# Token forms made in the tail before, output tiles finished in pairs, down chunks shifted by one pair, norm inside the third unit

## The chip, the cores and the metric

One core of a Trainium2 chip runs the whole program in one launch. TensorE (PE) multiplies, VectorE (DVE), ScalarE (ACT) and GpSimd (POOL) prepare operands and empty the accumulation banks, and SyncE (SP) issues every transfer. The metric is the device time of one execution in microseconds, the median of several; lower is better.

## The reference

The model is a decoder trunk of two layers over 512 tokens with 1024 features, in float32. Each layer is a token mixer between two half-step SwiGLU feed-forward networks (FFNs):

```python
def rms_norm(x, gain):
    y = x * lax.rsqrt(jnp.mean(x * x, axis=-1, keepdims=True) + RMS_EPS)
    return y * gain
def swiglu(x, w_gate, w_up, w_down):          # 1024 -> 2816 -> 1024
    return (jax.nn.silu(x @ w_gate) * (x @ w_up)) @ w_down
# x = x + 0.5 * swiglu(rms_norm(x))  before and after every mixer
```

Layer 0 mixes by dilated attention and causal pooling (one input and one output projection), layer 1 by an mLSTM with an input projection of 32 tiles and an output projection. So there are four FFNs, f = 0 to 3, in the order FFN 0, even mixer, FFN 1, FFN 2, odd mixer, FFN 3.

## The kernel before

**Layout and precision.** Activations stand with features on the partitions: `X` is 8 tiles of 128 features by 512 tokens. Every float32 operand is split into a high part (made by ACT) and a low part (made by DVE or POOL), and a product is three matmuls: high by high, high by low, low by high. A *unit* is one weight tile of 1024 by 128, loaded by SP into one of four ring slots (`RAW`), split into `HI` and `LO`, and multiplied with the 8 k-tiles of `XH` and `XL`: 24 matmuls of 512 columns into one bank (`products`, L504 to L506). A slot is loaded again when its unit is done.

**The FFN in blocks.** FFNs 1, 2 and 3 run in `block_ffn`. Of their 22 gate and up pairs the first 3 (`PLAIN`) are two plain units each, the other 19 are blocks: `block(p)` forms both outputs with seven half-size products in place of eight (L583 to L585: 84 matmuls of 256 columns). For it the kernel makes *token forms* `BF` and `BFL` once per FFN (`form_inputs` and `form_split` on ACT, `form` and `form_split` on DVE, a = 0 to 3, where form a needs the tiles a and 4 + a of X), and for each block sums of the weights (`ASR`, split to `ASH` and `ASL`). DVE puts the products together (`MID`), then `gate`, `up`. The sixteen blocks p = 4 to 19 are each followed by an *early* down product (`early`, L634 to L636: 24 matmuls of 512 columns, weights `DRAW` split to `DHI` and `DLO`), which adds 4 of the 22 hidden tiles to 2 of the 8 output tiles.

**The tail.** The last 6 hidden tiles go through the *tail*: 8 units of 6 k-tiles, one per output tile. After each, in this order on DVE: `residual_tile` (X, L1413), `new_x_tile` (XL, L1394, which waits for XH from ACT), then the split of the next weight tile (LO, L1448). ACT makes XH, the square and HI for each; POOL adds the squares.

**The start of a stage.** `two_units` runs the first two units side by side for 7 of the 8 k-tiles, so that the last tile of X may come late, and then their eighth; `norm(r)` adds up the squares with two matmuls (L533, L534), which wait for `SQL` (DVE L1399). ACT takes the root, DVE the reciprocal (`RSTD`), and only then can the banks of the first units be emptied. The order on DVE in `block_ffn` is written out by hand: form 0, SQL, form 1, split 0, form 2, split 1, norm, then splits, gates, ups, form 3 and the sums of block 3.

Each engine runs its list in order, so an instruction that waits holds up everything behind it on its engine.

Of the kernel before, what the change touches and what calls it, by code (L numbers as in the profile page):

```python
# [25 lines left out]
F32 = mybir.dt.float32  # L26
# [38 lines left out]
PLAIN = 3  # L65
BLOCKS = FT - PLAIN
EARLY = 16
TH_ = T // 2
# [73 lines left out]
def trunk(nc, xT, par_d, cst_d, hot_d, relb_d, w3_d, wgr_d, poolw_d, pick_d, gu_d, down_d, down2_d, ein_d, eout_d,  # L142
          oin_d, oout_d, skew_d, out_d):
    ctx = ExitStack()
    with ctx:
# [93 lines left out]
        BFR = at("BFR", [P, 4, 4, TH_], e0, 8 * TB)  # L239
        BFL = at("BFL", [P, 4, 4, TH_], e0, 8 * TB, F32R)  # L240
        ASR = at("ASR", [P, 2, 4, T], e0, 16 * TB)
        ASL = at("ASL", [P, 2, 4, T], e0, 16 * TB, F32R)
# [65 lines left out]
        sum_made, sum_hi, sum_lo = sem("sum_made"), sem("sum_hi"), sem("sum_lo")  # L308
        early_in, early_hi, early_lo, early_done, early_half, early_free = (
# [47 lines left out]
        def block_count(f, p):  # L357
            return BLOCKS * (f - 1) + p - PLAIN

        def early_count(f, p):  # L360
            return EARLY * (f - 1) + p - 4

        def has_early(p):
            return 4 <= p < 4 + EARLY

# [9 lines left out]
        def _(sp):  # L375
# [34 lines left out]
            def block_ffn(f, q0, after):  # L410
                base = 4 * q0

                def load_early(p):
                    e = early_count(f, p)
                    if p == 4:
                        sp.wait_ge(unit_done, base + 4)
                    if e:
                        sp.wait_ge(early_done, e)
                    m, c = 2 * ((p - 4) % 4), (p - 4) // 4
                    first = c % 2 * 4 * P  # L420
                    sp.dma_start(DRAW[:].rearrange("p (m c) -> p m c", m=2),
                                 down_d[f, 8 * (c // 2) + m:8 * (c // 2) + m + 2, :, first:first + 4 * P]
                                 .rearrange("m p c -> p m c")).then_inc(early_in, 16)

                for n in range(SLOTS, NU):
                    u = n if n < 2 * PLAIN else n ^ 1
                    load(q0 + n // 4, n % 4, gu_d[f, u])
                    p = n // 2 - 1
                    if n % 2 and has_early(p):
                        load_early(p)  # L430
                for m in range(KX):
                    load(q0 + (NU + m) // 4, m % 4, down2_d[f, m])
# [45 lines left out]
            projection(Q_OIN, 8, oin_d, oout_d)  # L478
            projection(Q_OOUT, 4, oout_d, gu_d[3])
            block_ffn(3, Q_FFN[3], None)  # L480
            for m in range(KX):

                sp.wait_ge(bank_free, 4 * Q_END - 8 + m + 5)
                sp.dma_start(out_d[:, m, :], X[:, m, :]).then_inc(out_done, 16)
# [4 lines left out]
        def _(pe):  # L489
# [26 lines left out]
            def x_tile_ready(r):  # L516
                return lambda k: pe.wait_ge(xl_ready, 8 * r + k + 1)

            def two_units(q, ready):

                for n0, n1 in ((0, KX - 1), (KX - 1, KX)):
                    for j in range(2):
                        pe.wait_ge(lo_ready, 4 * q + j + 1)
                        pe.wait_ge(bank_free, 4 * q + j + 1)
                        products(j, j, list(range(KX)), n0, n1, xh, xl, ready if j == 0 else None)
# [1591 lines left out]
```

## Time and profile before

| | |
|---|---|
| median of 3 runs | 2039.08 us (2036.6 to 2039.21) |
| profiled execution, own time | 2038.16 us |
| its span, first to last instruction | 2036.4 us |
| PE busy | 1988.9 us, 98% |
| DVE busy | 1372.5 us, 67% |
| ACT, POOL busy | 41%, 24% |
| mean granted TensorE clock | 0.995 |

Busy time of PE is not its peak, since matmuls overlap. In rows of a timeline the first number is the start in the span, the second the duration in microseconds, and a bracket at the end gives the idle time before the instruction and what ended it.

### The profile page before, as it was taken

The numbers are of one execution on the slowest core, as the hardware profiler recorded it, in microseconds if no ns is written. First come the engines' busy times: TensorE is split into PE (matmuls) and PEld (weight loads), VectorE is DVE, ScalarE is ACT, GpSimd is POOL, SyncE is SP. The second block draws the span as 40 slices with busy tenths as digits, with TensorE's granted clock in tenths as the row PEclk, the third lists the DMA queues.
The fourth block names the chain that finished last, engine by engine and source line by source line (L and its number), as shares of the span: only waits on it lengthen the run. The fifth ranks groups of instructions, "written<-read, shape, count | busy, mean of one in ns | idle before, by whom it ended". The sixth has DMA issues, their size and how long they took to land.

```text
span 2036.4 us, 27535 instructions
## 1 busy us (share of the span) xinstructions
PE 1988.9 (98%) x11150; PEld 1707.1 (84%) x11150; DVE 1372.5 (67%) x1752; ACT 838.3 (41%) x1200; POOL 492.1 (24%) x358
## 2 busy tenths in 40 slices
PE   7999999999999999999999999999998999999999
PEld 6888888876778999987899998877775788899998
DVE  6333333645498888868888886883468848888884
ACT  5323223524563343335334334554545335433342
POOL 1202112133231211222122122254025512211211
PEclk9999999999999999999999999999999999999999
DMA  5232223421123233322333333222200223223323
GB/s 177 93 102 95 93 93 131 149 83 52 53 85 111 97 101 104 104 83 83 105 103 104 96 112 99 94 86 83 79 1 1 73 93 104 94 95 113 95 93 104
DMA packets 61898, 189.25 MB, mean 93 GB/s; under 512 B 6096, under 2 KB 6352, under 8 KB 61776
## 3 DMA queue, kind: packets, MB, share of 16 engines
q1 hardware_dynamic: 61776, 187.52, 28.0%
q8 instruction: 89, 1.46, 0.3%
q14 instruction: 33, 0.27, 0.0%
HBM read 182.78 MB, written 4.72 MB: 92 GB/s over the span
## 4 chain that ended last, share of the span: by engine, by line
PE 82%; DVE 10%; ACT 3%; issue 2%; DMA 1%; POOL 1%; POOLq 0%; SPq 0%; DVEq 0%; ACTq 0%
PE BANKS L504 12%; PE BANKS L506 11%; PE BANKS L505 11%; PE BANKS L583 8%; PE BANKS L585 8%; PE BANKS L584 8%; PE BANKS L634 4%; PE BANKS L635 4%; PE BANKS L636 4%; DVE LO L1448 2%; PE BANKS L931 1%; ACT HI L1055 1%; DVE ASL L1493 1%; PE BANKS L757 1%; DVE SQ L1809 1%
## 5 line engine op out<-in xcount | busy, mean ns | idle before, releaser
L1386 DVE TENSOR_TENSOR LO<-RING,HI 128x1024 fp32r<-128x1024 f32 (+1 forms) x136 | 174.7, 1284 | 343.8 <-ACT HI L993 343.6
L504 PE MATMUL BANKS<-XH,HI 128*128 128x512 f32 x880 | 345.5, 393 | 11.5 <-DVE XL L1394 11.4
L505 PE MATMUL BANKS<-XL,HI 128*128 128x512 f32 x880 | 343.6, 391 | 0.0
L506 PE MATMUL BANKS<-XH,LO 128*128 128x512 f32 x880 | 343.5, 390 | 0.0
L1956 POOL TENSOR_TENSOR TMP<-TMP,RSTD 128x512 f32<-128x512 f32 x66 | 102.4, 1551 | 652.1 <-ACT TMP L1077 652.1
L993 ACT ACTIVATE HI<-RING 128x1024 fp32r<-128x1024 f32 (+1 forms) x144 | 150.2, 1044 | 228.7 <-DMA RING<-gu_dram 95.5
L504 PEld LDWEIGHTS BANKS<-XH,HI 128*128 128x128 f32 x880 | 165.9, 189 | 51.8 <-DVE LO L1386 11.0
L583 PE MATMUL BANKS<-BF,ASH 128*128 128x256 f32 x684 | 195.0, 285 | 4.6 <-DVE ASL L1493 4.4
L506 PEld LDWEIGHTS BANKS<-XH,LO 128*128 128x128 f32 x880 | 165.8, 188 | 34.9
L505 PEld LDWEIGHTS BANKS<-XL,HI 128*128 128x128 f32 x880 | 166.0, 189 | 34.0
L585 PE MATMUL BANKS<-BF,ASL 128*128 128x256 f32 x684 | 194.3, 284 | 0.0
L584 PE MATMUL BANKS<-BFL,ASH 128*128 128x256 f32 x684 | 194.3, 284 | 0.0
L1448 DVE TENSOR_TENSOR LO<-RING,HI 128x1024 fp32r<-128x1024 f32 (+2 forms) x152 | 158.8, 1045 | 31.3 <-ACT HI L1055 31.1
L1077 ACT ACTIVATE TMP<-TMP 128x512 f32<-128x512 f32 x66 | 41.7, 632 | 302.0 <-DVE TMP L1503 301.7
L634 PE MATMUL BANKS<-HH,DHI 128*128 128x512 f32 x384 | 152.3, 397 | 6.1 <-DVE DLO L1552 6.1
L635 PE MATMUL BANKS<-HL,DHI 128*128 128x512 f32 x384 | 151.9, 395 | 0.0
L636 PE MATMUL BANKS<-HH,DLO 128*128 128x512 f32 x384 | 151.3, 394 | 0.0
L1493 DVE TENSOR_TENSOR ASL<-ASR,ASH 128x1024 fp32r<-128x1024 f32 x114 | 141.5, 1243 | 0.0
L583 PEld LDWEIGHTS BANKS<-BF,ASH 128*128 128x128 f32 x684 | 132.2, 193 | 5.7 <-DVE ASL L1493 5.7
L583 PE MATMUL BANKS<-XH,HI 128*128 128x256 f32 x456 | 129.3, 284 | 4.1 <-DVE LO L1448 4.0
L584 PEld LDWEIGHTS BANKS<-BFL,ASH 128*128 128x128 f32 x684 | 132.2, 193 | 0.0
L585 PEld LDWEIGHTS BANKS<-BF,ASL 128*128 128x128 f32 x684 | 132.1, 193 | 0.0
(254 smaller groups left out, 4729.1 us busy)
## 6 DMA issues: line engine op xcount, KB each, us to landing
RING<-gu_dram SPq DMA_DIRECT2D x176, 512.0 KB, 3.4
DRAW<-down_dram SPq DMA_DIRECT2D x48, 512.0 KB, 3.8
RING<-oin_dram SPq DMA_DIRECT2D x32, 512.0 KB, 3.4
RING<-down_dram SPq DMA_DIRECT2D x32, 384.0 KB, 3.1
RING<-down_dram SPq DMA_DIRECT2D x16, 512.0 KB, 3.4
RING<-ein_dram SPq DMA_DIRECT2D x16, 512.0 KB, 3.4
RING<-oout_dram SPq DMA_DIRECT2D x16, 512.0 KB, 3.4
RING<-eout_dram SPq DMA_DIRECT2D x8, 512.0 KB, 3.8
```

The lines of the kernel that those rows point to most:

```text
L504: pe.matmul(PS[bank][:], HI[j][:, c], hi(k), start=(n == 0), stop=False)
L505: pe.matmul(PS[bank][:], HI[j][:, c], lo(k), start=False, stop=False)
L506: last = pe.matmul(PS[bank][:], LO[j][:, c], hi(k), start=False, stop=(n == len(order) - 1))
L583: pe.matmul(out, w_hi[:, c], x_hi(k), start=(k == 0), stop=False)
L584: pe.matmul(out, w_hi[:, c], x_lo(k), start=False, stop=False)
L585: last = pe.matmul(out, w_lo[:, c], x_hi(k), start=False, stop=(k == 3))
L634: pe.matmul(bank, DHI[:, col], HH[:, h, :], start=(k == 0), stop=False)
L635: pe.matmul(bank, DHI[:, col], HL[:, h, :], start=False, stop=False)
L636: last = pe.matmul(bank, DLO[:, col], HH[:, h, :], start=False, stop=(k == 3))
L1386: dve.tensor_tensor(LO[j][:, 0:kt * P], RAW[j][:, 0:kt * P], HI[j][:, 0:kt * P].bitcast(F32), ALU.subtract).then_inc(lo_ready, 1)
L1448: dve.tensor_tensor(LO[j][:, cols], RAW[j][:, cols], HI[j][:, cols].bitcast(F32), ALU.subtract).then_inc(lo_ready, 1)
L1493: dve.tensor_tensor(ASL[:, p % 2, 2 * i:2 * i + 2, :], ASR[:, p % 2, 2 * i:2 * i + 2, :], ASH[:, p % 2, 2 * i:2 * i + 2, :].bitcast(F32), ...
```

## The change

- `PLAIN` becomes `(None, 4, 3, 3)`: FFN 1 has four plain pairs and 18 blocks, FFNs 2 and 3 stay at three and 19.
- Early down products begin with the first block (`PLAIN[f]`) and still last sixteen blocks. `LATE = (None, 6, 7, 7)`: in FFNs 2 and 3 the tail takes 7 hidden tiles, and the first four early products take 3 instead of 4. Chunks that cross the border of two weight arrays are loaded in two transfers, and each late weight tile of FFNs 2 and 3 in two (64 KB and 384 KB, the first counted on `late_in`).
- From FFN 1's tail on, output tiles are finished in the order `PAIRED = (0, 4, 1, 5, 2, 6, 3, 7)`, also in both output projections' consumers, and PE takes the k-tiles in that order.
- Forms 0 to 2 and the splits 0 and 1 of FFN 2 are made in the tail of FFN 1, those of FFN 3 in the second half of the odd mixer's output projection (`forms_behind`). `BFR`/`BFL` and `ASR`/`ASL` exchange their places in memory.
- `start_of_stage` replaces `two_units` and `norm`: the norm's two matmuls stand behind the first 3 k-tiles of the third unit, in all six stages that have a norm.
- At the end of the even mixer two weight splits stand behind the last tile of XL instead of between the tiles.

```diff
-PLAIN = 3
-BLOCKS = FT - PLAIN
+PLAIN = (None, 4, 3, 3)
 EARLY = 16
+LATE = (None, 6, 7, 7)
+PAIRED = (0, 4, 1, 5, 2, 6, 3, 7)
...
+        def early_tiles(f, p):
+            c, first = (p - PLAIN[f]) // 4, FT - LATE[f] - 12
+            return range(first) if c == 0 else range(first + 4 * c - 4, first + 4 * c)
...
+            def start_of_stage(q, r):
                 for n0, n1 in ((0, KX - 1), (KX - 1, KX)):
                     for j in range(2):
...
+                        products(j, j, x_order(r), n0, n1, xh, xl, x_tile_ready(r) if j == 0 else None)
+                unit_with_norm(q, r)
+
+            def unit_with_norm(q, r):
+                pe.wait_ge(lo_ready, 4 * q + 3)
+                pe.wait_ge(bank_free, 4 * q + 3)
+                products(2, 2, list(range(KX)), 0, 3, xh, xl)
+                norm(r)
+                products(2, 2, list(range(KX)), 3, KX, xh, xl)
...
+            def forms_behind(f, m):          # ACT: form_inputs and form_split, DVE: form and form_split
+                if m in (2, 4, 6):
+                    form(f, m // 2 - 1)
+                if m in (3, 5):
+                    form_split(f, m // 2 - 1)
...
                 for m in range(KX):                       # the tail of block_ffn on DVE
                     residual_tile(q0 + (NU + m) // 4, m % 4, r, m, 0.5)
                     if m < 4:
-                        split(NU + 4 + m, slice(0, 6 * P))
+                        split(NU + 4 + m, late)
                     elif after:
                         split(NU + 4 + m, whole)
+                    if f == 1:
+                        forms_behind(2, m)
...
+                else:                                     # the start on DVE for f = 2 and 3
+                    squares_low(now)
+                    form_split(f, 2)
+                    form(f, 3)
+                    form_split(f, 3)
+                    norm(now)
+                    split(4, whole)
+                    gate(0)
+                    up(0)
+                    split(5, whole)
+                    gate(1)
+                    sums_first(first)
+                    up(1)
...
                     if m:                                 # the end of the even mixer on DVE
                         new_x_tile(2, m - 1)
-                        if m % 2 == 0:
-                            if m == 2:
-                                dve.wait_ge(lo_ready, N_ATTN + 4)
-                            split_unit(N_ATTN + m // 2 + 3)
+                        if m == 2:
+                            dve.wait_ge(lo_ready, N_ATTN + 4)
+                            split_unit(N_ATTN + 4)
+                        elif m == 4:
+                            split_unit(N_ATTN + 5)
+                split_unit(N_ATTN + 6)
+                split_unit(N_ATTN + 7)
```

## Rows read from the trace of the kernel before

**Rows 1.** The page's first part: busy time and share, PE.

```profile
PE 1988.9 (98%) x11150; PEld 1707.1 (84%) x11150; DVE 1372.5 (67%) x1752; ACT 838.3 (41%) x1200; POOL 492.1 (24%) x358
```

**Rows 2.** Waits of PE: total us, times, longest.

```profile
PE BANKS L504 <- DVE XL L1394: 11.4, 2, 10.2
...
PE BANKS L634 <- DVE DLO L1552: 6.1, 3, 2.0
PE BANKS L583 <- DVE ASL L1493: 4.4, 3, 1.7
PE BANKS L583 <- DVE LO L1448: 4.0, 2, 2.7
...
PE BANKS L533 <- DVE SQL L1399: 2.0, 3, 1.3
...
PE BANKS L504 <- POOL HL L1958: 1.0, 3, 0.3
```

**Rows 3.** Windows at FFN starts: length; PE, PEld, DVE, ACT, POOL; clock; DMA.

```profile
567.72:632.85 65.13, 58.11 (x322) 50.04 (x321) 58.61 (x71) 34.19 (x46) 18.77 (x12) 0.97 0.27 89
919.39:991.05 71.66, 64.42 (x339) 55.54 (x338) 61.24 (x74) 36.38 (x49) 19.09 (x13) 0.93 0.27 89
1680.26:1746.57 66.31, 61.60 (x339) 53.30 (x338) 57.65 (x71) 33.02 (x45) 17.50 (x11) 0.97 0.28 95
```

**Rows 4.** Timeline of PE at the start of FFN 2.

```profile
919.39 0.39 PE L504 MATMUL BANKS<-XH,HI 128*128 128x512 f32 x1
919.62 0.39 PE L505 MATMUL BANKS<-XL,HI 128*128 128x512 f32 x1
...
957.24 0.39 PE L583 MATMUL BANKS<-XH,HI 128*128 128x256 f32 x1 [2.72 <-DVE LO L1448]
...
960.59 0.58 PE L583 MATMUL BANKS<-BF,ASH 128*128 128x256 f32 x1 [1.02 <-DVE ASL L1493]
...
981.43 0.28 PE L584 MATMUL BANKS<-BFL,HI 128*128 128x256 f32 x1
981.55 0.28 PE L585 MATMUL BANKS<-BF,LO 128*128 128x256 f32 x1
983.87 0.50 PE L634 MATMUL BANKS<-HH,DHI 128*128 128x512 f32 x1 [2.04 <-DVE DLO L1552]
...
985.42 0.63 PE L634 MATMUL BANKS<-HH,DHI 128*128 128x512 f32 x1
985.85 0.63 PE L635 MATMUL BANKS<-HL,DHI 128*128 128x512 f32 x1
```

**Rows 5.** Timeline of DVE, tail of FFN 1 and start of FFN 2.

```profile
922.14 0.75 DVE L1394 SCALAR_TENSOR_TENSOR XL<-X,PAR,XH 128x512 fp32r<-128x512 f32 x1 [0.80 <-ACT XH L1000]
...
926.53 0.75 DVE L1394 SCALAR_TENSOR_TENSOR XL<-X,PAR,XH 128x512 fp32r<-128x512 f32 x1 [0.79 <-ACT XH L1000]
...
929.44 0.47 DVE L1454 SCALAR_TENSOR_TENSOR BFR<-X,PAR,MID 128x256 f32<-128x256 f32 x1
...
930.96 0.68 DVE L1399 TENSOR_TENSOR SQL<-SQ,SQH 128x512 fp32r<-128x512 f32 x1
...
933.77 1.22 DVE L1466 TENSOR_TENSOR BFL<-BFR,BF 128x1024 fp32r<-128x1024 f32 x1
...
957.10 3.43 DVE L1493 TENSOR_TENSOR ASL<-ASR,ASH 128x1024 fp32r<-128x1024 f32 x2
```

**Rows 6.** Timeline of POOL, start of FFN 2.

```profile
957.32 2.14 POOL L1956 TENSOR_TENSOR TMP<-TMP,RSTD 128x512 f32<-128x512 f32 x1 [1.22 <-ACT TMP L1077]
```

**Rows 7.** Timeline of DVE, end of the odd mixer's output projection.

```profile
1685.00 1.22 DVE L1386 TENSOR_TENSOR LO<-RING,HI 128x1024 fp32r<-128x1024 f32 x1 [2.10 <-ACT HI L993]
```

**Rows 8.** Timeline of DVE, blocks 20 and 21 of FFN 2.

```profile
1227.30 0.42 DVE L1518 TENSOR_TENSOR MID<-BANKS,MID 128x256 f32<-128x256 f32 x1 [2.11 <-PE BANKS L585]
...
1239.31 0.41 DVE L1518 TENSOR_TENSOR MID<-BANKS,MID 128x256 f32<-128x256 f32 x1
```

**Rows 9.** DMA issues: KB each, median us to landing.

```profile
DRAW<-down_dram SPq DMA_DIRECT2D x48, 512.0 KB, 3.8
```

More of the change, by code:

```diff
@@ L852, in odd_mixer @@
                 q0 = Q_OIN
-                two_units(q0, x_tile_ready(4))
-                norm(4)
-                for j in range(2, SLOTS):
-                    unit(q0, j, KX, xh, xl)
+                start_of_stage(q0, 4)
+                unit(q0, 3, KX, xh, xl)
                 def bank(item):
@@ L1115, in block_ffn @@
+                split(2 * first, whole)
+                sums_split(first, 0)
+                sums_split(first, 1)
+                split(2 * first + 1, right)
+                silu(first - 1, 1.0)
+                h_high(first - 1)
+                for p in range(first, FT):
                     nxt = p + 1 if p + 1 < FT else None
                     copy_one(p)
-                    if p > PLAIN and not has_early(p - 1):
+                    if p > first and not has_early(f, p - 1):
                         h_high(p - 1)
@@ L1576, in block_ffn @@
-                form_split(3)
-                sums_first(PLAIN)
-                up(1)
-                sums_second(PLAIN)
-                sums_third(PLAIN)
-                dve.wait_ge(sum_made, 3 * block_count(f, PLAIN) + 3)
-                gate(2)
-                split(6, whole)
-                sums_split(PLAIN, 0)
-                sums_split(PLAIN, 1)
-                split(7, right)
-                up(2)
-                for p in range(PLAIN, FT):
+                now, first, late = (2, 3, 5)[f - 1], PLAIN[f], slice(0, LATE[f] * P)
@@ new lines, in block_ffn @@
+                if f == 1:
+                    form(f, 0)
+                    squares_low(now)
+                    form(f, 1)
+                    form_split(f, 0)
+                    form(f, 2)
+                    form_split(f, 1)
+                    norm(now)
+                    split(4, whole)
+                    gate(0)
+                    form(f, 3)
+                    form_split(f, 2)
+                    up(0)
+                    split(5, whole)
+                    gate(1)
+                    form_split(f, 3)
+                    up(1)
+                    split(6, whole)
+                    split(7, whole)
+                    gate(2)
+                    up(2)
+                    sums_first(first)
+                else:
+                    squares_low(now)
+                    form_split(f, 2)
+                    form(f, 3)
+                    form_split(f, 3)
+                    norm(now)
+                    split(4, whole)
+                    gate(0)
+                    up(0)
+                    split(5, whole)
+                    gate(1)
+                    sums_first(first)
+                    up(1)
@@ L1589, in block_ffn @@
+                sums_second(first)
+                sums_third(first)
+                dve.wait_ge(sum_made, 3 * block_count(f, first) + 3)
+                gate(first - 1)
+                split(2 * first, whole)
+                sums_split(first, 0)
+                sums_split(first, 1)
+                split(2 * first + 1, right)
+                up(first - 1)
+                for p in range(first, FT):
                     nxt = p + 1 if p + 1 < FT else None
-                    if has_early(p):
+                    if has_early(f, p):
@@ L1633, in block_ffn @@
                         gate(p)
[L1634 removed]
+                        split(NU + 2, late)
                         up(p)
[L1636 removed]
+                split(NU + 3, late)
                 for m in range(KX):
```

304 lines of the change are left out of this document (165 added, 139 removed).

## The prediction

> **What bounds the kernel now.** I read the page first: PE is busy for 1988.9 us, 98% of the span [rows 1], so a gain can only come from the 47 us in which it is idle, from a lower clock, or from fewer matmuls. Next PE's waits [rows 2]: apart from the wait for the first data (10.2 of the 11.4 for XL) the larger ones name DVE, and the three for DLO, the three for ASL and the two for LO belong to `block_ffn`, which runs three times. The windows of the three starts [rows 3] show the same: DVE is busy 58.6 of 65.1, 61.2 of 71.7 and 57.7 of 66.3 us while PE goes without work, and the mean clock is 0.97, 0.93, 0.97. In steady blocks no such wait occurs. The bound is therefore DVE's list at three starts, PE everywhere else.
>
> **The rates.** From neighbouring starts [rows 4]: a 512-column matmul starts every 0.2275 us (919.39 to 919.62, rounded), a 256-column one every 0.12, and at half clock a 512-column one every 0.43. So a unit is 24 x 0.2275 = 5.46, a block 84 x 0.12 = 10.08, a plain pair 10.92. Reading the start-to-start times over each start, what exceeds those rates (idle time, restart of about 0.1, lower clock) is 10.2 us for FFN 1, 12.6 for FFN 2, 7.6 for FFN 3. About 1.6, 3.5 and 1.5 of it is clock; the windows' clocks times their lengths give 2, 5 and 2 [rows 3], coarser because rounded.
>
> **FFN 1.** The fourth plain pair gives DVE one more pair (10.9 us of PE work for about 3.5 us of its own: two splits, a gate, an up) before block sums are wanted, and it removes block 3 with its sums. The forms stay at this start. Going through DVE's list with the old durations, the split sums of block 4 are ready about 1 us before PE wants them; the early product's DLO comes about 0.5 us late, because the second weight tile of block 5 is loaded only after the last plain unit. The XL wait of 1.2 [rows 2] goes with the weight split (1.1 us on DVE) moved behind the XL tiles; 0.15 is left. Cost: 10.92 - 10.08 = 0.84 more matmul time. Gain 10.2 - 0.15 - 0.6 - 0.84 = 8.6; it would be 7.0 if one half-clock stretch came back, 9.2 with no wait left.
>
> **FFN 2, the doubtful part.** The forms go into FFN 1's tail, and there DVE is not idle in a useful sense: tile by tile it goes X, wait for XH, XL, wait for HI, LO, next X, a chain of 4.1 to 4.4 us per tile between DVE and ACT, while PE needs 18 x 0.2275 = 4.1. It ends late as it is: PE begins FFN 2 at 919.39 [rows 4], the seventh XL tile starts at 922.14, the eighth at 926.53 [rows 5]. A form is 929.44 to 930.96 = 1.52 us, a form split 1.22 less 0.09 of overlap = 1.13. They stand between LO and the next X, so they add to the chain: 2 forms and 2 splits = 5.3 before the seventh tile, a third form = 6.8 before the eighth. The seventh XL is then ready at 922.14 + 0.75 + 5.3 = 928.2; PE wants it after six k-tiles, at 919.39 + 18 x 0.2275 = 923.5. **PE waits 4.7 us at a place where it waits for nothing now**, then 0.4 for the eighth (928.2 + 0.7 + 4.8 = 933.7 against 934.1). A wait of 2.0 is followed by half clock here (983.87, then 0.43 from 985.42) [rows 4], so I add one such stretch, 1.6. Behind that, DVE's list from form 0 to the last split sum takes 929.44 to 960.53 [rows 5], and is 6.8 shorter by the same forms while it starts 6.8 later: the second product of block 3, now at 960.59, comes at about 961.4. So the waits up to there (norm, LO, ASL: 6.5 with restarts and 0.5 of clock) buy nothing. What is gained lies behind: the half clock from 960.6 on (1.7 with restart), 0.4 at MID, 2.3 for DLO, 1.4 of clock, since early products already follow block 3 and DVE keeps its lead; less 0.8 for the later product and about 0.3 for DLO in block 3. Gain 4.8. Bounds: 11.5 if the tail had room, 0 if the forms took longer and the clock stayed low longer (rivals).
>
> At the last step DVE and POOL matter together: two ASL splits of 1.22 each take 3.43 [rows 5] beside POOL's 2.14 us multiply [rows 6], so about 1.1 is lost to it. In the tail a form follows LO, after POOL's add has ended, and I charge nothing. The Trainium skill (SBUF — State Buffer, Who interferes with whom) says that a DVE instruction with two SBUF inputs and a GpSimd instruction that reads SBUF exclude each other for a whole instruction, whoever starts first. The trace agrees in the two rows named. By that rule alone each of the three forms could lose up to 1.1 in the tail and FFN 2's gain would be 1.5 instead of 4.8; the order in the list speaks against it.
>
> **FFN 3.** Here the forms go behind the output projection's units of 24 matmuls. DVE has 2.10 us of idle time before each LO [rows 7], more than a form (1.52), so the delay doesn't add up: only the last form moves the eighth XL by 1.5, and the two side-by-side units hide that. DVE's list at the start is 6.8 shorter, the norm comes 9 x 0.2275 = 2.05 later than now, and the sums must wait for the fourth unit's slot to be reloaded; split sums are ready about 0.7 before PE's second product. The waits for LO, ASL, MID and DLO with their clock go, about 0.6 at the first DLO stays. Gain 7.0; 5.4 with one half-clock stretch.
>
> **Norm in the third unit.** Where PE waits for SQL it now has 2.05 us of work. Start of the kernel and odd mixer: the SQL waits are 2.0 in all, 1.3 of them FFN 2's [rows 2], so 0.7, with restarts 1.2. The cover: the root comes up to 2 us later, but between norm and the fifth unit lie 39 matmuls = 8.9 us, against about 8 us for root, reciprocal, first scaling and split. Were the cover gone, each of six norms would cost at most 2.05.
>
> **Tail of FFNs 2 and 3.** With 7 k-tiles the two first units run 36 matmuls before they need the last hidden tile instead of 30: of three waits for HL two go, 0.7, with restarts 1.2. Matmuls are the same in number. But three blocks without early product now follow each other (19, 20, 21) in place of two. Such a block takes DVE 1227.30 to 1239.31 = 12.0 us [rows 8] against PE's 10.08, so DVE falls 1.9 behind once more; block 21's split sums are late by 0 to 1.9, I take 1.2: twice, minus 2.4.
>
> **Transfers.** Four early chunks in each of FFNs 2 and 3 come in two pieces. One piece lands in 3.8 us [rows 9]; the split of DRAW starts some 5 us after the buffer is free, so I charge nothing; two pieces strictly after each other would land at 7.6 and cost about 1 us each, 8 in all.
>
> **Sum.** 8.6 + 4.8 + 7.0 + 1.2 + 1.2 - 2.4 = 20.4 us. The profiled execution took 2038.16, its span 2036.4 with 1.8 around it: 2017.8. The median of the runs lies 0.9 above it: 2018.7, I say 2018.5.
>
> **Rivals.**
> - *The tail has room* (0.12): the chain with ACT absorbs the forms, no wait at the seventh XL. For it: DVE is idle 0.5 to 0.8 twice a tile. Against it: those gaps are waits within the chain, not at its end. FFN 2 gains 11.5: 2012.
> - *The tail costs more* (0.17): the wait for XL is 7 or more and the clock is low for twice as long, FFN 2 gains 0: 2023.5.
> - *Covers fail elsewhere* (0.08): transfers in two pieces late (8 us) or block 21 late by the full 1.9: 2027.
> - *No difference* (0.04): a moved wait simply turns up at the next early product in all three FFNs, since DVE is busy 90% of each start. Against it: block 3's sums and the forms do leave those windows. 2036.
> - *Slower* (0.04): the two-piece transfers. They decide from the point where the second piece lands more than 2.6 us later than DRAW's split can bear, 20.4 / 8; at one full extra latency each with PE's clock halved after each wait (2 + 1.6 + 1 per block) the loss is 37: 2055. No row shows two pieces on one counter.
>
> The forecast itself has 0.55, its own range 2013 to 2023. The range 2011 to 2027 takes in the first three rivals' times and leaves out no more than 0.2. A difference under 0.2% (4 us) can't be told from none: faster 0.91, same 0.05, slower 0.04.
>
> **What the profile after should show.** PE waits: a new one for XL of 4 to 5 us in FFN 2's first unit (right) or none (the tail has room); ASL, LO and DLO together under 4 us instead of 14.5; no SQL. PE clock 1.0 in FFN 1's and FFN 3's starts, below it in FFN 2's. An ASL wait near block 21 of FFNs 2 and 3. FFN 1's window from its first unit to the first full block after the first early product shorter by about 8.6. The prediction is wrong if early products wait for DHI (transfers), or if FFNs 1 and 3 still show half clock at their starts.

## The result and the profile after

The changed kernel takes **2022.93 us** (median of 4 runs, 2021.86 to 2023.61). The kernel before took 2038.8 beside it (4 runs, 2036.6 to 2039.21). The ratio is 0.9924, its 95% interval 0.9907 to 0.9941: 15.9 us faster where 20.4 was forecast. The profiled execution took 2022.40 us, 15.8 less than that of before, so its trace can stand for the difference.

The page's first part and PE's waits (total us, times, longest), to be laid beside [rows 1] and [rows 2]:

```profile
PE 1982.1 (98%) x11114; PEld 1701.4 (84%) x11114; DVE 1364.1 (68%) x1742; ACT 836.8 (41%) x1197; POOL 492.4 (24%) x358
```

```profile
PE BANKS L538 <- DVE XL L1466: 15.0, 3, 10.1
...
PE BANKS L626 <- DVE ASL L1573: 3.9, 4, 1.2
...
PE BANKS L676 <- DVE DLO L1633: 1.8, 3, 0.9
...
PE BANKS L626 <- DVE LO L1546: 0.5, 2, 0.3
PE BANKS L538 <- POOL HL L2065: 0.3, 1, 0.3
```

ASL, LO and DLO came to 14.5 us and now come to 6.2; SQL is gone, of three HL waits one is left. XL grew from 11.4 to 15.0: 10.1 is the first data as before, the new part is one wait of 4.35 us. Of the 3.9 for ASL, 2.4 stand at block 21 of FFNs 2 and 3, where nothing waited before. The windows of the three starts (length; PE, PEld, DVE, ACT, POOL; clock; DMA), against [rows 3]:

```profile
566.98:625.26 58.28, 56.53 (x286) 47.84 (x285) 52.15 (x61) 31.74 (x43) 16.11 (x11) 1.00 0.29 100
911.77:982.28 70.51, 64.55 (x352) 55.31 (x350) 57.97 (x71) 35.48 (x47) 19.23 (x12) 0.98 0.29 94
1669.42:1732.33 62.91, 62.00 (x352) 54.42 (x350) 51.36 (x62) 29.16 (x40) 16.88 (x11) 1.00 0.32 105
```

FFN 1's window is 65.13 - 58.28 = 6.85 us shorter. The two others hold 12 matmuls more of 512 columns than before (two early products of 18 in place of one of 24), 2.7 us, so their lengths can't be compared directly. FFN 2's wait and its clock, in PE's timeline (start, duration, bracket: idle time before and what ended it):

```profile
915.62 0.39 PE L540 MATMUL BANKS<-XH,LO 128*128 128x512 f32 x1
920.36 0.80 PE L538 MATMUL BANKS<-XH,HI 128*128 128x512 f32 x1 [4.35 <-DVE XL L1466]
...
922.66 0.63 PE L540 MATMUL BANKS<-XH,LO 128*128 128x512 f32 x1
923.09 0.60 PE L538 MATMUL BANKS<-XH,HI 128*128 128x512 f32 x1
923.51 0.40 PE L539 MATMUL BANKS<-XL,HI 128*128 128x512 f32 x1
```

922.66 to 923.09 is the 0.43 of half clock, from 923.51 on the full one is back.

As in the prediction, I read the starts of all matmuls of one profiled execution and summed what exceeds the three rates of the prediction. This sum is called *excess* below: it holds idle time, the restart after it and lower clock. In these terms the gain is made up so:

| term | before | after | gain | forecast |
|---|---|---|---|---|
| FFN 1's start, less 0.84 for the longer pair | 9.99 | 2.29 | 6.9 | 8.6 |
| FFN 2's start | 12.62 | 8.77 | 3.85 | 4.8 |
| FFN 3's start | 7.45 | 1.32 | 6.1 | 7.0 |
| norm, start of the kernel and odd mixer | | | 1.4 | 1.2 |
| HL waits in two tails | | | 1.15 | 1.2 |
| block 21, FFNs 2 and 3 | 0 | 3.6 | -3.6 | -2.4 |
| sum | | | 15.8 | 20.4 |

### The profile page after: what moved, and what is told of

Read it like the earlier page. It is cut to its first block, busy times and chain, and to the rows that moved or that the text cites. A ratio compares the mean times of both kernels' runs of the same rounds, so it can differ in the third digit from the quotient of the medians.

```text
span 2020.7 us, 27444 instructions
## 1 busy us (share of the span) xinstructions
PE 1982.1 (98%) x11114; PEld 1701.4 (84%) x11114; DVE 1364.1 (68%) x1742; ACT 836.8 (41%) x1197; POOL 492.4 (24%) x358
## 4 chain that ended last, share of the span: by engine, by line
PE 85%; DVE 9%; ACT 2%; issue 2%; POOL 1%; DMA 1%; SPq 0%; DVEq 0%; POOLq 0%; ACTq 0%
PE BANKS L538 13%; PE BANKS L539 13%; PE BANKS L540 13%; PE BANKS L626 9%; PE BANKS L628 9%; PE BANKS L627 9%; PE BANKS L676 4%; PE BANKS L677 4%; PE BANKS L678 4%; PE BANKS L970 1%; DVE LO L1546 1%; DVE LO L1457 1%; DVE XC L1858 1%; PE BANKS L798 1%; DVE SQ L1914 1%
## 5 line engine op out<-in xcount | busy, mean ns | idle before, releaser
L538 PE MATMUL BANKS<-XH,HI 128*128 128x512 f32 x896 | 352.4, 393 | 15.1 <-DVE XL L1466 15.0
L539 PE MATMUL BANKS<-XL,HI 128*128 128x512 f32 x896 | 350.3, 391 | 0.0
L540 PE MATMUL BANKS<-XH,LO 128*128 128x512 f32 x896 | 350.2, 391 | 0.0
L1546 DVE TENSOR_TENSOR LO<-RING,HI 128x1024 fp32r<-128x1024 f32 (+3 forms) x152 | 163.0, 1072 | 34.6 <-ACT HI L1116 34.5
L676 PE MATMUL BANKS<-HH,DHI 128*128 128x512 f32 x368 | 144.1, 392 | 1.8 <-DVE DLO L1633 1.8
L677 PE MATMUL BANKS<-HL,DHI 128*128 128x512 f32 x368 | 143.7, 391 | 0.0
L678 PE MATMUL BANKS<-HH,DLO 128*128 128x512 f32 x368 | 143.2, 389 | 0.0
L1116 ACT ACTIVATE HI<-RING 128x1024 fp32r<-128x1024 f32 (+3 forms) x152 | 126.3, 868 | 16.6 <-DMA RING<-down_dram 16.6
L538 PE MATMUL BANKS<-HH,HI 128*128 128x512 f32 x336 | 130.8, 389 | 0.3 <-POOL HL L2065 0.3
L539 PE MATMUL BANKS<-HL,HI 128*128 128x512 f32 x336 | 130.7, 389 | 0.0
```

Of the source, the lines that this page charges most:

```text
L538: pe.matmul(PS[bank][:], HI[j][:, c], hi(k), start=(n == 0), stop=False)
L539: pe.matmul(PS[bank][:], HI[j][:, c], lo(k), start=False, stop=False)
L540: last = pe.matmul(PS[bank][:], LO[j][:, c], hi(k), start=False, stop=(n == len(order) - 1))
L676: pe.matmul(bank, DHI[:, col], HH[:, h % 8, :], start=(k == 0), stop=False)
L677: pe.matmul(bank, DHI[:, col], HL[:, h % 8, :], start=False, stop=False)
L678: last = pe.matmul(bank, DLO[:, col], HH[:, h % 8, :], start=False, stop=(h == tiles[-1]))
```

## The experiments

Twelve kernels ran. The e's below are edits of the changed kernel, but for e9, which is an edit of e7, and e12, one of e9. Times of one kernel spread over 1.8 to 5.5 us (up to 6.6 for the kernel before), and much of that is not at the places studied. Between 1290 and 1600 us PE works on the mLSTM of the odd mixer, which no edit touches, and the excess there was 49.2 to 54.2 us by profiled execution. These are windows of that stretch with seven late tiles in FFN 1 (first row) and with four plain pairs and the gate moved (second):

```profile
1290.00:1600.00 310.00, 298.23 (x1363) 229.19 (x1362) 208.93 (x226) 157.02 (x239) 111.42 (x88) 0.98 0.16 51
```

```profile
1290.00:1600.00 310.00, 297.07 (x1382) 228.75 (x1381) 211.47 (x227) 156.91 (x240) 120.14 (x92) 1.00 0.16 53
```

The clock is 0.98 against 1.00 of 310 us; from 1500 to 1600 us alone it is 0.93 and 1.00, so some 14 us at half clock against none. The other executions lie between, and their excess in the mLSTM follows the clock. The runs of one kernel show the same: those of e2 took 2023.01 us at a mean clock of 0.997 and 2017.67 at 1.0. So a kernel's place is read from its excess at the starts, and its time says whether that holds. The excess is that of one execution each. Where two kernels have the same instructions at a start it agrees within 0.3 us, even at FFN 2's start (8.77 to 8.96 in the changed kernel, e4, e5 and e11), although half clock behind the XL wait lasts twice as long in e4. The kernels ran in five groups on several chips, the changed one, e1 to e4, e5 to e8, e9 to e11 and e12, each group beside the kernel before: across groups the ratios compare better than the medians. All in us; ratios are to the kernel before, each beside its own runs of it; "block 21" is the excess at that block of FFN 2 (FFN 3 has as much again).

| kernel | median | ratio, 95% | FFN 1 | FFN 2 | block 21 | mLSTM | FFN 3 |
|---|---|---|---|---|---|---|---|
| before | 2038.8 | 1 | 9.99 | 12.62 | 0 | 50.2 | 7.45 |
| changed | 2022.93 | 0.9924 (0.9907 to 0.9941) | 2.29 | 8.77 | 1.8 | 50.3 | 1.32 |
| e1 | 2021.44 | 0.9916 (0.9902 to 0.9929) | 2.11 | 7.04 | 1.8 | 53.2 | 1.41 |
| e2 | 2020.75 | 0.9909 (0.9895 to 0.9922) | 2.02 | 6.01 | 1.8 | 54.2 | 1.34 |
| e3 | 2028.97 | 0.9954 (0.9940 to 0.9967) | 2.19 | 12.50 | 0 | 50.5 | 3.93 |
| e4 | 2032.34 | 0.9970 (0.9957 to 0.9982) | 8.71 | 8.96 | 1.8 | 49.2 | 1.43 |
| e5 | 2024.72 | 0.9932 (0.9915 to 0.9948) | 2.14 | 8.89 | 1.8 | 51.4 | 1.48 |
| e6 | 2017.99 | 0.9897 (0.9880 to 0.9913) | 1.89 | 3.60 | 1.8 | 51.7 | 1.41 |
| e7 | 2012.39 | 0.9868 (0.9852 to 0.9885) | 2.02 | 1.11 | 0 | 51.8 | 0.97 |
| e8 | 2017.95 | 0.9891 (0.9875 to 0.9908) | 1.87 | 4.73 | 0 | 54.2 | 1.05 |
| e9 | 2014.41 | 0.9888 (0.9872 to 0.9903) | 2.38 | 1.17 | 0 | 49.9 | 1.34 |
| e10 | 2025.65 | 0.9941 (0.9927 to 0.9954) | 2.59 | 9.65 | 1.8 | 51.8 | 2.02 |
| e11 | 2023.98 | 0.9931 (0.9917 to 0.9944) | 2.13 | 8.79 | 1.8 | 50.6 | 2.57 |
| e12 | 2011.11 | 0.9863 (0.9846 to 0.9880) | 1.66 | 0.63 | 0 | 50.3 | 0.11 |

(Four plain pairs cost 0.84 of matmul time per FFN: in FFN 1 in all kernels but before and e4, in FFNs 2 and 3 in e7, e8, e9 and e12.)

**e1: FFN 2's forms back at its own start.**

```diff
-                    if f == 1:
-                        forms_behind(2, m)
...
+                elif f == 2:
+                    form(f, 0)
+                    squares_low(now)
+                    form(f, 1)
+                    form_split(f, 0)
+                    form(f, 2)
+                    form_split(f, 1)
+                    norm(now)
+                    split(4, whole)
+                    gate(0)
+                    form(f, 3)
+                    form_split(f, 2)
...
```

The first two lines are in the tail, on ACT and DVE; the others are DVE's list at the start, and ACT's changes likewise.

> The changed kernel, but all four token forms of FFN 2 are made at the start of FFN 2 again (none in FFN 1's tail); everything else stays, the order of tiles and the shifted down chunks included. In the changed kernel FFN 2's start costs 8.9 us over the rates, 4.9 of it the wait for the seventh XL tile and about 1.3 the half clock behind it. Theory (the forms in this tail nearly pay for themselves and no more): the XL wait and its clock go, but DVE's list at the start is 6.8 us longer, so LO, ASL and DLO are late by 2 to 3 us each again; excess of 11 to 12 us, 2 to 3.5 us slower than the changed kernel, 2025 to 2026.5. Rival 1 (the forms in the tail are a net loss, the other parts gain): excess 7 or less, 2021 or less. Rival 2 (they are the whole gain of FFN 2 and more): 4 us or more slower, above 2027.

My theory fell. The first rival came nearest and missed both its bounds by a hair (7.04 for 7, 2021.44 for 2021): the excess is 1.7 less than in the changed kernel. The XL wait is gone. In its place stand one of 1.29 for the bank of the third pair's first unit (DVE's gate 0) and one for LO with half clock behind it. In FFN 2 neither ASL nor DLO is late:

```profile
948.88 0.58 PE L626 MATMUL BANKS<-XH,HI 128*128 128x256 f32 x1 [2.73 <-DVE LO L1561]
```

The times alone (ratios 0.9916 and 0.9924) can't tell the two kernels apart. By the excess the forms in FFN 1's tail save nothing.

The XL rows show why. With forms in the tail (changed kernel), then without (e1):

```profile
902.84 0.75 DVE L1466 SCALAR_TENSOR_TENSOR XL<-X,PAR,XH 128x512 fp32r<-128x512 f32 x1 [0.79 <-ACT XH L1039]
908.10 0.75 DVE L1466 SCALAR_TENSOR_TENSOR XL<-X,PAR,XH 128x512 fp32r<-128x512 f32 x1 [0.79 <-ACT XH L1039]
914.03 0.75 DVE L1466 SCALAR_TENSOR_TENSOR XL<-X,PAR,XH 128x512 fp32r<-128x512 f32 x1 [0.79 <-ACT XH L1039]
919.55 0.75 DVE L1466 SCALAR_TENSOR_TENSOR XL<-X,PAR,XH 128x512 fp32r<-128x512 f32 x1 [0.79 <-ACT XH L1039]
925.47 0.75 DVE L1466 SCALAR_TENSOR_TENSOR XL<-X,PAR,XH 128x512 fp32r<-128x512 f32 x1 [0.80 <-ACT XH L1039]
```

```profile
905.01 0.75 DVE L1481 SCALAR_TENSOR_TENSOR XL<-X,PAR,XH 128x512 fp32r<-128x512 f32 x1 [0.79 <-ACT XH L1039]
909.40 0.75 DVE L1481 SCALAR_TENSOR_TENSOR XL<-X,PAR,XH 128x512 fp32r<-128x512 f32 x1 [0.79 <-ACT XH L1039]
913.78 0.75 DVE L1481 SCALAR_TENSOR_TENSOR XL<-X,PAR,XH 128x512 fp32r<-128x512 f32 x1 [0.79 <-ACT XH L1039]
918.17 0.75 DVE L1481 SCALAR_TENSOR_TENSOR XL<-X,PAR,XH 128x512 fp32r<-128x512 f32 x1 [0.79 <-ACT XH L1039]
```

Without forms a tile takes 4.39 us where PE takes 4.10: DVE falls behind by 0.29 per tile anyway. With forms the steps are 5.26, 5.93, 5.52 and 5.92: the two splits add 0.87 and 1.13, the two forms 1.54 and 1.53, so nearly all of their own length (1.13 and 1.52). None of them lost a further 1.1, as a DVE split does beside POOL's multiply in [rows 5] and [rows 6]. The last XL stands 13.7 us behind PE's first matmul of FFN 2 (911.77) with forms, 6.9 without (911.29): 6.8 later, as the prediction had it.

**e2: seven late tiles in FFN 1 too.** `EFIRST` says where early products begin; the high part of hidden tiles 11, 15 and 19 is made one block later.

```diff
-LATE = (None, 6, 7, 7)
+LATE = (None, 7, 7, 7)
+EFIRST = (None, 4, 3, 3)
...
-                    if has_early(f, p):
+                    if not high_later(f, p):
                         h_high(p)
```

> The changed kernel with 7 late hidden tiles in FFN 1 too, so that PE needs 21 matmuls = 4.78 us for each tile of the tail in place of 4.10 (as many matmuls in all; its early products still begin with block 4, and three high parts of hidden tiles are made one block later so that their slots are free). Theory (the XL wait of 4.5 us is the excess of DVE's chain of 4.1 to 4.4 us per tile plus forms over PE's time per tile): each of four or more tiles gives DVE 0.68 us more, the wait for the seventh tile falls by about 2.7 to 1.8, the HL wait in FFN 1's tail (0.5, with restart 0.6) goes, the half clock goes or halves: 3.7 to 5 us faster than the changed kernel, 2018 to 2019.5. Rival 1 (the chain hangs on PE's own time through the banks, so it stretches along): wait stays above 4, only the HL wait goes, 2022.3. Rival 2 (twelve more two-piece transfers or the late high parts cost): waits for DHI or HL in FFN 1's blocks, above 2023.

```profile
917.11 0.50 PE L543 MATMUL BANKS<-XH,HI 128*128 128x512 f32 x1 [1.58 <-DVE XL L1471]
```

The wait fell from 4.35 to 1.58 (1.8 expected), there is no half clock behind it, the HL wait is gone, nothing waits for DHI: 3.4 us less excess from 700 us on. The wait is thus DVE's chain against PE's time per tile: it fell by 2.77 where four tiles of 0.68 more make 2.7. The median fell by 2.2 only, where 3.7 to 5 were expected, and the intervals overlap; 3.9 of the profiled execution went to the mLSTM.

**e3: no shift of the down chunks.**

```diff
-LATE = (None, 6, 7, 7)
+LATE = (None, 6, 6, 6)
+EFIRST = (None, 4, 4, 4)
```

> The changed kernel without the shift of the down chunks: early products begin with block 4 in all three FFNs, four hidden tiles each, 6 late tiles, one transfer per chunk. Theory (three blocks in a row without early product cost DVE its lead, wherever they lie; DVE takes 12.0 us for such a block, PE 10.08): the waits at block 21 (1.85 and 1.84 with restarts) go and the first DLO waits (0.9 and 1.2) move, two HL waits come back (1.2), but block 3 now puts DVE 1.9 us further behind at block 4, twice: about the same as the changed kernel, 2022 to 2024. Rival 1 (the shift is only a cost): 4 us faster, 2018.5. Rival 2 (the shift is what gains behind block 3): waits of over 2 us each for DLO at block 4 with half clock behind them, 4 us or more slower, above 2027.

```profile
973.49 0.39 PE L627 MATMUL BANKS<-BF,HI 128*128 128x256 f32 x1 [0.75 <-DVE MID L1605]
...
977.22 0.50 PE L677 MATMUL BANKS<-HH,DHI 128*128 128x512 f32 x1 [2.04 <-DVE DLO L1634]
...
1728.89 0.50 PE L677 MATMUL BANKS<-HH,DHI 128*128 128x512 f32 x1 [2.04 <-DVE DLO L1634]
```

```profile
973.02 0.41 DVE L1605 TENSOR_TENSOR MID<-BANKS,MID 128x256 f32<-128x256 f32 x1
973.36 1.21 DVE L1547 TENSOR_TENSOR LO<-RING,HI 128x1024 fp32r<-128x1024 f32 x1
974.49 0.41 DVE L1611 TENSOR_TENSOR MID<-BANKS,MID 128x256 f32<-128x256 f32 x1
974.82 1.21 DVE L1574 TENSOR_TENSOR ASL<-ASR,ASH 128x1024 fp32r<-128x1024 f32 x1
975.96 1.21 DVE L1634 TENSOR_TENSOR DLO<-DRAW,DHI 128x1024 fp32r<-128x1024 f32 x1
```

The second rival stood, but for the half clock that it saw behind the waits: there is none. The waits at block 21 went, which shows that three blocks in a row make them and two don't; but 2.04 us for DLO came back, the same figure as in [rows 2] (three waits, longest 2.0) and [rows 4]. It is the same whatever went before, because PE and DVE meet late in the block: PE waits for DVE's MID (973.49), has 1.41 us of work left from there (to its last start at 974.90), and DVE's list from that MID to the end of DLO takes 4.15 (973.02 to 977.17). In FFN 1 of the kernel before the same stretches are 621.91 to 623.32 for PE and 621.44 to 625.59 for DVE. The shift is worth 6 us by the times and 3.9 by the excess. Up to 1.3 of the 3.9 may be chance: half clock lasts twice as long behind the XL wait here. It does so in e4 too, which has the shift, and there the FFN costs 0.2 more in the end.

**e4: three plain pairs in FFN 1.**

```diff
-PLAIN = (None, 4, 3, 3)
+PLAIN = (None, 3, 3, 3)
+EFIRST = (None, 4, 3, 3)
...
```

The lists of ACT and DVE at this start lose the fourth pair with it.

> The changed kernel with three plain pairs in FFN 1 as before (forms at its start, early products from block 4). The changed kernel's FFN 1 start costs 2.6 us over the rates and 0.84 for the longer pair. Theory (the fourth pair is what gains there, by 10.9 us of PE work against 3.5 of DVE's own): of the 10.2 us before, only the XL wait (0.7) and the gap at norm are gone, waits for LO, ASL and DLO are back; 5 to 6.5 us slower than the changed kernel, 2028 to 2029.5. Rival (norm inside the third unit and the moved weight splits make up most of it): 1 to 2 us slower, 2024 to 2025.

By the excess the theory stood: 8.71 against 2.29 + 0.84, 5.6 us for the fourth pair; LO, ASL and DLO (2.04 again) are late as before. The profiled execution took 2027.79, 5.4 more than the changed kernel's. The five others took 2031 to 2033, so the median is 9.4 us slower, more than the 5 to 6.5 expected. Their mean clock was 0.994 to 0.996, that of the profiled one 0.997, which can make 2 to 6 us; where it was lower the one trace doesn't show.

**e5: norm before the third unit.**

```diff
-                products(2, 2, list(range(KX)), 0, 3, xh, xl)
                 norm(r)
-                products(2, 2, list(range(KX)), 3, KX, xh, xl)
+                unit(q, 2, KX, xh, xl)
```

> The changed kernel with the norm's two matmuls before the third unit again, in all six stages. Theory (SQL comes up to 2 us after the first two units and three k-tiles of work cover it): waits for SQL return, 0.7 us in all at the start of the kernel and the odd mixer and about 1.3 in FFN 2, with restarts 2 to 2.5; no wait is less than in the changed kernel, since the root's chain had room. 1 to 2.5 us slower, 2024 to 2025.5. Rival (the root and what hangs on it was late by those 2 us, the block sums above all): the waits at the starts, 1.3 us at block 4 of FFN 1 and 2.7 behind the norm in FFN 2, shrink by more than SQL costs: same or faster, 2020 to 2022.9.

```profile
24.29 0.47 PE L573 MATMUL BANKS<-SQH,SELR 128*128 128x512 f32 x1 [1.15 <-DVE SQL L1468]
```

1.8 us slower by the medians, with overlapping intervals. The trace has 1.4 at norm in the kernel's start, but only 0.4 to 1.0 over the first 40 us (3.3 in e5 and in the kernel before, 2.3 to 2.9 in the others); 0.3 in the even mixer and 0.1 in FFN 2. None of the starts got better, so norm inside the third unit is covered, as the theory had it. The rest of the theory failed: it had waits for SQL in FFN 2 (1.3) and in the odd mixer too, and there is only the one above. In FFN 2 PE is itself late by the XL wait. In e1, where it isn't, DVE ends SQL at 923.29, 1.1 us after PE begins the third unit, and there the new place covers a wait.

**e6: both, seven late tiles and forms at the start.** Edits of e1 and e2 together.

> Seven late tiles in FFN 1 and the forms of FFN 2 at its start, three plain pairs there. FFN 2's start cost 8.8 us over the rates in the changed kernel, 7.0 with its forms at the start, 6.0 with seven late tiles and the forms in the tail. Theory (with 4.78 us per tile DVE leaves the tail earlier against PE, and a list without forms in the tail ends it without any XL wait): excess 4 to 5.5, 2018.5 to 2020. Rival (DVE's list from the start of FFN 2 on sets the sums whatever the tail): excess 7 as with six late tiles, 2021.

FFN 2's start costs 3.60, less than the theory's 4 to 5.5. The XL and bank waits are gone, LO keeps 1.46. What FFN 2 lacked was time to leave FFN 1's tail, not room in its own list: against e1 the slower tail saves 3.4 us, and against e2 (6.01) the forms back in the list save 2.4.

**e7 and e8: four plain pairs everywhere, FFN 2's forms at the start or in the tail.**

```diff
-PLAIN = (None, 4, 3, 3)
+PLAIN = (None, 4, 4, 4)
...
-LATE = (None, 6, 7, 7)
+LATE = (None, 7, 7, 7)
+EFIRST = (None, 4, 4, 4)
...
-                if f == 1:
+                if f < 3:
                     form(f, 0)
...
```

The last lines are in e7 only: there FFNs 1 and 2 share one list.

> Four plain pairs, early products from block 4 and seven late tiles in all three FFNs; FFN 1's and FFN 2's forms at their own start, FFN 3's in the output projection. Theory (10.9 us of PE work against 3.5 of DVE's is what a start wants; two blocks without early product in a row cost no wait, three do): FFN 2's start costs 2.4 us as FFN 1's, no wait at block 21, FFN 3's start under 0.8; plus 0.84 of matmuls twice: 9 to 10 us faster than the changed kernel, 2013 to 2014. Rival (the fourth pair only moves the wait to the first early product): waits for DLO of 1 us or more in FFNs 2 and 3, 2017 or more.

> The same with FFN 2's forms in the tail of FFN 1, as in the changed kernel. Theory (with four plain pairs the list at the start has room, so a form in the tail only costs): an XL wait of 1.8 us and 0.5 and 1.0 behind it stay, all that the forms' removal from the list gives is under 2.3; same as the kernel with forms at the start or up to 2.5 us slower, 2014 to 2016. Rival (the list at the start is still what is late): faster than that kernel, 2012 or less.

PE's waits in e7, XL with only the first data of the kernel (10.1) and 0.5 in FFN 1:

```profile
PE BANKS L543 <- DVE XL L1473: 10.6, 2, 10.1
...
PE BANKS L631 <- DVE ASL L1580: 1.6, 2, 1.0
...
PE BANKS L681 <- DVE DLO L1640: 1.1, 2, 0.8
```

2012.39, 10.5 faster than the changed kernel where 9 to 10 were expected. e8 has 3.6 us more excess in FFN 2, with the XL wait of 1.54; more than the 2.5 expected at most, the same sign. Its median is 5.6 above e7's, and the profiled executions differ by 6.5, 2.4 of it in the mLSTM. The forms in this tail are a loss in all three pairs of kernels, of 1.7 (e1), 2.4 (e6 against e2) and 3.6 us (e7 against e8): the more room the start has, the greater.

**e9 and e10: the gate behind the split sums**, on e7 and on the changed kernel.

```diff
-                gate(first - 1)
                 split(2 * first, whole)
                 sums_split(first, 0)
                 sums_split(first, 1)
+                gate(first - 1)
```

> The kernel with four plain pairs, seven late tiles and FFN 2's forms at its start, and in addition DVE's gate of the last plain pair placed behind the two splits of the first block's sums in all three FFNs (it stood ahead of the weight split before them). In that kernel PE still waits 1.18 and 0.74 for the second ASL split, which takes 2.32 us beside POOL's multiply of 1.94 where it takes 1.22 alone, and POOL's multiply follows from this gate. Theory (DVE and POOL hold each other up there, and the gate stands ahead of what PE wants first): both ASL waits go, 2.0 with restarts, and DLO is up to 0.7 earlier: 2 to 3.5 us faster, 2009 to 2010.5. Rival (the multiply meets another DVE instruction later and the first early product waits by as much more): DLO waits grow by 1 each, no gain, 2012 to 2013.

> The same single edit on the changed kernel (four, three, three plain pairs). There PE waits 1.17 for ASL in FFN 1, 0.74 in FFN 2, 0.15 to 0.26 at the fourth product of block 3 in FFNs 2 and 3, and 0.4, 0.8 and 1.1 for DLO. Theory as above: the ASL waits go in FFNs 1 and 2 (2.1 with restarts) and DLO gains up to 0.5 each: 2 to 3.5 us faster than the changed kernel, 2019.5 to 2021. That would say that 1.8 of the gain missing in FFN 1 was lost to POOL. Rival: no gain, DLO waits grow, 2022.9.

DVE and POOL in the changed kernel, FFN 1 (the first row is both splits together, the second the later of them):

```profile
607.05 3.46 DVE L1573 TENSOR_TENSOR ASL<-ASR,ASH 128x1024 fp32r<-128x1024 f32 x2
608.18 2.32 DVE L1573 TENSOR_TENSOR ASL<-ASR,ASH 128x1024 fp32r<-128x1024 f32 x1
```

```profile
607.49 1.94 POOL L2063 TENSOR_TENSOR TMP<-TMP,RSTD 128x512 f32<-128x512 f32 x1 [3.50 <-ACT TMP L1126]
```

And in e10, DVE (the first row is both splits together), POOL and PE:

```profile
606.18 2.35 DVE L1573 TENSOR_TENSOR ASL<-ASR,ASH 128x1024 fp32r<-128x1024 f32 x2
...
611.21 0.69 DVE L1592 TENSOR_TENSOR TMP<-BANKS,TMP 128x512 f32<-128x512 f32 x1 [1.48 <-POOL TMP L2063]
```

```profile
609.88 1.30 POOL L2063 TENSOR_TENSOR TMP<-TMP,RSTD 128x512 f32<-128x512 f32 x1 [6.16 <-ACT TMP L1126]
```

```profile
612.89 0.39 PE L626 MATMUL BANKS<-BF,ASH 128*128 128x256 f32 x1 [0.75 <-ACT MID L1137]
```

The mechanism was right: apart from each other the split takes 1.2 us and the multiply 1.30, together 2.32 and 1.94, and the ASL wait in FFN 1 is gone (in e10 that of 0.6 in FFN 2 stays, against the forecast). The gain was not there. DVE now stands idle for 1.48 before `up`, until POOL is done, and ACT copies product one to MID only behind the high part that waits for this `up`. The wait moved from the second product to the fourth and to DLO. The excess at the three starts is 1.9 us more in e10 than in the changed kernel and 0.8 more in e9 than in e7. The medians are 2.7 and 2.0 above theirs, with overlapping intervals, where 2 to 3.5 less were expected. The rival stood in both (no gain), with ACT's queue as a part that I had not seen.

**e11: FFN 3's forms at its own start.** The edit of e1 for f == 3; `forms_behind(3, ...)` leaves the output projection.

> The changed kernel with all forms of FFN 3 at FFN 3's own start (none behind the output projection). FFN 3's start costs 1.4 us over the rates in the changed kernel; FFN 2's costs 7.0 with its forms at the start and the same lists. Theory (behind units of 24 matmuls DVE has 2.1 us of idle time per tile, so the forms cost nothing there and their whole relief of the start is kept): excess 6 to 7.5, 4.5 to 6 us slower than the changed kernel, 2027.5 to 2029. Rival (as in FFN 2 the relief is given back, here by later XL and norm): within 1.5 us, 2021.5 to 2024.5.

Excess 2.57 against 1.32, 1.3 us and the rival's range; the theory had 6 to 7.5. That is the second surprise: three forms and two splits, 6.8 us of DVE's list, are hidden almost whole in the list at this start. DVE's rows show where. First the changed kernel, then e11:

```profile
1683.73 3.35 DVE L1475 RECIPROCAL RSTD<-RSTD 128x512 f32<-128x512 f32 x1 [0.89 <-ACT RSTD L1053]
...
1696.06 1.23 DVE L1555 TENSOR_TENSOR ASR<-RING 128x1024 f32<-128x1024 f32 x1 [2.61 <-DMA RING<-gu_dram]
```

```profile
1683.66 3.35 DVE L1490 RECIPROCAL RSTD<-RSTD 128x512 f32<-128x512 f32 x1
```

The reciprocal begins at the same time with the forms in the list and without. Without them DVE waits before it for ACT, and 2.61 us more for the transfer of the weight tile that the sums need.

**e12: the first early split ahead**, on e9.

```diff
                 split(2 * first + 1, right)
+                early_high(first)
                 silu(first - 1, 1.0)
+                copy_one(first)
                 h_high(first - 1)
...
                 split(2 * first + 1, right)
+                early_split(first)
                 up(first - 1)
```

The first part is ACT's list, the second DVE's. For this block the three calls fall away at their later places.

> The kernel with four plain pairs and the gate behind the split sums, and in addition: ACT copies the first block's product one (MID) before it makes the last plain pair's high part instead of behind it, and the first early product's DHI and DLO are made by ACT and DVE before the last plain pair's silu and up, in the 1.5 us in which DVE waits for POOL there. Without these two PE waited 0.9 and 0.4 for MID and 0.8, 0.8 and 1.2 for DLO, and the ASL waits had gone. Theory (what bounds a start now is DVE's list up to the first DLO, in which POOL costs either 1.1 of longer splits or 1.5 of idle time; an edit that only moves the wait gains nothing, one that fills the idle time does): MID and DLO waits of the first early products go, PE's excess behind 560 us falls from 5.5 (4.7 with the gate ahead) to about 1.5; 3 to 4 us faster than the kernel with the gate ahead, if the projections' own spread of 2 us allows to see it: 2008.5 to 2011. Rival (the split ahead delays the up and with it the sums of the second block, whose split sums are then late): an ASL or LO wait of 1 us at the second block in each FFN, 2011 to 2013.

```profile
PE BANKS L543 <- DVE XL L1479: 10.9, 2, 10.5
...
PE BANKS L681 <- DVE DLO L1646: 1.1, 2, 0.6
```

DVE's rows in FFN 1:

```profile
610.29 0.95 DVE L1646 TENSOR_TENSOR DLO<-DRAW,DHI 128x768 fp32r<-128x768 f32 x1
612.43 0.69 DVE L1605 TENSOR_TENSOR TMP<-BANKS,TMP 128x512 f32<-128x512 f32 x1 [1.19 <-POOL TMP L2080]
```

DLO now comes before `up`, in place of 619.15 in e9. The idle time before `up` is not gone: POOL's multiply lies beside this split, `up` comes 0.6 later than in e9 (612.43 for 611.83), and 1.19 of the 1.48 is left. No wait for ASL or MID over 0.3 is left, and the first early product waits no more in any FFN; FFNs 1 and 2 wait 0.57 for DLO at the second one, a mild form of the rival. Excess at the three starts is 2.40 against 4.10 in e7. The median 2011.11 is the lowest of all, 1.3 below e7 where 3 to 4 were expected, and the intervals don't separate them; against the changed kernel it is 11.8 us.

## Why the prediction was right, and where it was off

The time (2022.93) lies in the range and is nearer to 2018.5 than to the kernel before; every term came with its sign. The mechanism came too: a wait for the seventh XL tile of 4.35 us (4 to 5 forecast), clock 1.00 in the windows of FFNs 1 and 3 and 0.98 in FFN 2's, an ASL wait at block 21, no wait for DHI. One sign was missed: ASL, LO and DLO together came to 6.2 us for "under 4", 2.4 of it at block 21. The 4.6 us that are missing are sizes of terms:

- **FFN 1, 8.6 forecast, 6.9 measured.** "The split sums of block 4 are ready about 1 us before PE wants them": they cost 1.17, wait and restart. I had gone through DVE's list with old durations; at this place POOL's multiply lies beside the last split (2.32 for 1.22) and `up` waited twice for POOL (1.18 and 2.06). e10 shows the 1.1, and also that it isn't to be had by moving the gate. The DLO wait was 0.4 for 0.6; the XL rest 0.67 for 0.15, since XL tiles back to back take up to 1.79 us beside POOL's squares. e4 prices the fourth pair at 5.6 of this.
- **FFN 2, 4.8 and 3.85.** The wait at the seventh tile was 4.51 for 4.7, its half-clock stretch and restart 1.55 for 1.6, the eighth tile cost nothing for 0.4. What was wrong is what stands behind it: LO 0.57 and ASL 0.84 at block 3 where I had charged a later product of 0.8, 0.36 more at its fourth product, DLO 0.88 for 0.3.
- **FFN 2's forms.** The prediction set a cost of 6.7 in the tail (4.7, 0.4 and 1.6) against 6.5 of waits that go before the second product of block 3, and so found that the forms buy nothing up to there. They lose: e1 costs 1.7 less. It put the gain behind that point, on early products that follow block 3 already, and e3 bears this out: without the shift the excess is 12.50, against 12.62 before, up to 1.3 of it by the longer half clock.
- **FFN 3, 7.0 and 6.1.** "About 0.6 at the first DLO stays": 1.18. Here the account is off: the shorter list of DVE was to take away the waits for LO, ASL, MID and DLO, but the forms behind the output projection give 1.3 (e11), the shift 2.6 (e3) of it. The rest, some 2.2, no run took apart, so that the sum came near for this FFN is in part luck.
- **Block 21, -2.4 and -3.6.** "0 to 1.9, I take 1.2": 1.8 each. The cause stands by e3 and e7 (no wait there with two such blocks in a row). From MID to MID DVE takes 11.69 us for the first of these blocks (1200.26 to 1211.95) and 12.46 for the next (to 1224.41), against PE's 10.08.
- **Norm and HL** came in the forecast size: 1.4 and 1.15 for 1.2 and 1.2. Half of the first is not norm's new place: e5, which takes it back, has no wait in the odd mixer, where the kernel before had one of 0.6 with its restart. What else ended that one no run took apart. **Two-piece transfers** cost nothing: no wait for DHI in any kernel with them.

The rival "the tail has room" is out by the 4.35 us wait, "slower" by the absence of DHI waits, "no difference" by the 15.8 us less excess. Of "covers fail elsewhere" one half came, block 21 late by nearly the full 1.9, but it cost 1.2 us more than forecast and not 8. "The tail costs more" forecast this time (2023.5) almost to the microsecond, but for another reason: its XL wait of 7 didn't come, and FFN 2 gained 3.85 where it has 0. By the time alone it is the better forecast.

## What to carry to other kernels

Before work is moved out of a list that is late, compare the pace of where it goes: in a chain that takes 4.39 us per tile against 4.10 of the bound engine nearly every microsecond added arrives, while behind the output projection, with 2.1 us of idle time per tile, no wait for XL came of it. Then ask what the list gets back where it was: 6.8 us taken out of a list that also waits for the norm and for a weight tile gave 1.3. Where a wait is the same figure whatever came before (2.04 us for DLO, six times in the kernel before, e3 and e4), look for the last place where the two engines met: the wait is what the one's list from there takes beyond the other's work. Moving an instruction can move the wait, to other queues too (e9, e10). One more piece of the plain, cheap kind of work at each start was the largest single step: after its 0.84 us it gave 5.6 in FFN 1 (e4) and some 4.9 in FFNs 2 and 3 together (e7 against e6, both by excess; there it also puts an end to the three blocks in a row). All the rest of the change, the reordering, gave some 10.

## What the runs showed of the hardware

- A DVE split with two inputs in SBUF and a POOL multiply at the same time took 2.32 and 1.94 us; with the one edit that parts them 1.17 (two in 2.35) and 1.30, so 1.15 and 0.64 less. The rows fit engines that take turns: POOL began at 607.49, within the first split (607.05 to about 608.2), and 0.64 later that split was at its end; the second split began at 608.18, and from POOL's end at 609.43 its own 1.17 lead to 610.60, where it ended at 610.50. The Trainium skill (SBUF — State Buffer, Who interferes with whom) has it that only the shared pair of ports makes DVE and GpSimd hold each other up, and as an exclusive lock: these rows agree.
- The same instructions in the mLSTM cost 49.2 to 54.2 us over the rates from one execution to the next, by the granted clock (0.98 to 1.00 over 310 us). Two kernels that differ by 2 us can't be ranked by the times of one execution each. Their excess at the starts can, since it agrees within 0.3 us where the instructions are the same.
- After the XL wait of 4.35 us PE ran at half clock (1.2 of 2.4 GHz) for about 3 us, after 1.58 us at the same place not at all, after 2.73 us for LO in e1 again. The wait's length alone doesn't decide: behind the 2.04 us for DLO the clock fell all three times in the kernel before and not once in e3 (twice) and e4 (once).
